# Two RMS norms of a transformer block computed from three sums gathered during the output projection, the second root applied behind the up and gate products

## What is computed

```python
mix = hybrid_mixer(rms_norm(h, g_pre_mix), ...)      # ends with merged @ w_out
h = h + rms_norm(mix, g_post_mix)
ffn = conv_gated_mlp(rms_norm(h, g_pre_ffn), w_up_gate, conv_w_ffn, w_down)
h = h + rms_norm(ffn, g_post_ffn)

def rms_norm(x, g):    # over the 1024 features of a token
    return x * rsqrt(mean(x * x) + 1e-6) * g

def conv_gated_mlp(xn, w_up_gate, conv_w_ffn, w_down):
    u, g = split(xn @ w_up_gate, 2)                  # 2 x 2816 features
    u = causal_dwconv(u, conv_w_ffn)                 # 3 taps along the tokens
    return (gelu(u) * g) @ w_down
```

## Time and profile before

| | us |
|---|---|
| median of 3 runs (1785.23 to 1788.03) | 1786.21 |
| the profiled execution, its own time | 1784.76 |
| its span | 1783.0 |
| PE, DVE, ACT, POOL busy | 1720.4, 1039.9, 877.9, 357.9 |
| last job of the output projection read by ACT | at 668.65 |
| first matmul of the up product | at 694.82 |
| end of the last up and gate product | at 946.16 |

### The profile page before, as it was taken

One profiled execution on the slowest core, in us unless ns is written; L12 is line 12 of the kernel. 1 busy time (PEld: TensorE's weight loads), 2 busy tenths in 40 slices (PEclk: granted clock), 3 DMA queues, 4 the chain that ended last, 5 costly groups with the idle time before them and its releaser, 6 DMA issues.

```text
span 1783.0 us, 29994 instructions
## 1 busy us (share of the span) xinstructions
PE 1720.4 (96%) x11496; PEld 1548.2 (87%) x11496; DVE 1039.9 (58%) x1589; ACT 877.9 (49%) x1205; POOL 357.9 (20%) x520
## 2 busy tenths in 40 slices
PE   6999999998999998999999998999999999999996
PEld 6999999998999998999998887788777777888885
DVE  6655566654455566875653336576677676755443
ACT  6777677775333243333333223475655555633331
POOL 0111101010000025988814970000000000000001
PEclk9999999999999997999999997999999999999998
DMA  4111222122444442443434544764112212233332
GB/s 154 61 56 57 72 71 71 60 60 66 137 154 162 160 149 42 142 135 109 122 103 133 141 111 163 210 199 128 48 60 89 65 53 82 77 106 112 119 115 90
DMA packets 67942, 189.22 MB, mean 106 GB/s; under 512 B 15248, under 2 KB 19472, under 8 KB 67728
## 3 DMA queue, kind: packets, MB, share of 16 engines
q1 hardware_dynamic: 63936, 175.99, 31.7%
q0 software_dynamic: 3920, 12.06, 2.4%
HBM read 165.74 MB, written 19.92 MB: 104 GB/s over the span
## 4 chain that ended last, share of the span: by engine, by line
PE 85%; DVE 6%; ACT 4%; issue 2%; DMA 1%; SPq 0%; POOL 0%; ACTq 0%; DVEq 0%
PE J L883 34%; PE J L1132 18%; PE J L899 7%; PE J L1102 7%; PE J L1267 2%; PE J L1257 2%; PE J L1006 2%; PE Z L923 2%; PE J L1312 2%; PE Z L978 1%; DMA WR<-weights 1%; DVE MX L2416 1%; DVE WL L1870 1%; PE Z L968 1%; PE Z L991 1%
## 5 line engine op out<-in xcount | busy, mean ns | idle before, releaser
L1870 DVE TENSOR_TENSOR WL<-WR,WH 128x1024 fp32r<-128x1024 f32 x247 | 326.2, 1327 | 224.2 <-ACT WH L1396 215.9
L1396 ACT ACTIVATE WH<-WR 128x1024 fp32r<-128x1024 f32 x247 | 259.6, 1055 | 229.3 <-DMA WR<-weights 115.1
L883 PE MATMUL J<-XH,WH 128*128 128x258 f32 (+1 forms) x1376 | 282.0, 286 | 4.6 <-ACT XH L1432 2.0
L883 PE MATMUL J<-XH,WL 128*128 128x258 f32 (+1 forms) x1376 | 279.0, 284 | 0.0
L883 PE MATMUL J<-XL,WH 128*128 128x258 f32 (+1 forms) x1376 | 273.8, 283 | 0.0
L883 PEld LDWEIGHTS J<-XH,WH 128*128 128x128 f32 x1376 | 216.4, 191 | 9.3 <-issue 6.8
L883 PEld LDWEIGHTS J<-XH,WL 128*128 128x128 f32 x1376 | 214.2, 190 | 0.0
L883 PEld LDWEIGHTS J<-XL,WH 128*128 128x128 f32 x1376 | 212.0, 189 | 0.1
L2558 POOL TENSOR_TENSOR SA<-SQ 128x512 f32<-128x512 f32 (+1 forms) x3 | 4.9, 1620 | 688.9 <-ACT SQ L1655 493.3
L2540 POOL TENSOR_SCALAR_AFFINE_SELECT E<-E 128x128 f32<-128x128 f32 (+2 forms) x160 | 48.2, 338 | 386.8 <-DVE E L1954 223.9
L1954 DVE SCALAR_TENSOR_TENSOR E<-Z,E 128x1348 f32<-128x1348 f32 x16 | 25.0, 1562 | 85.3 <-ACT E L1468 85.3
(11 more groups left out here) (438 smaller groups left out, 4152.5 us busy)
## 6 DMA issues: line engine op xcount, KB each, us to landing
WR<-weights SPq DMA_DIRECT2D x247, 512.0 KB, 3.6
AW<-weights SPq DMA_DIRECT2D x24, 512.0 KB, 4.5
CPS<-cp_dram SPq DMA_DIRECT2D x8, 576.0 KB, 6.7
cp_dram<-CQR POOLq DMA_DIRECT2D x16, 144.0 KB, 3.0
cp_dram<-CQI POOLq DMA_DIRECT2D x16, 144.0 KB, 2.9
X<-tokens SPq DMA_DIRECT2D x4, 528.0 KB, 5.1
H<-tokens SPq DMA_DIRECT2D x8, 264.0 KB, 4.7
bp_dram<-BQR POOLq DMA_DIRECT2D x8, 256.0 KB, 2.3
```

The source lines that it names most:

```text
L883: mm = pe.matmul(o[:, 512 * h:512 * h + half], ws[:, s, w], xs[:, a:a + half], start=(k == 0 and i == 0 and part != WITH_LOW), stop=(k == ...
L1396: act.activation(WH[:, n % SPLIT, :], WR[:, n % RAW, :], ACT.Copy).then_inc(w_hi, 1)
L1870: dve.tensor_tensor(WL[:, n % SPLIT, :], WR[:, n % RAW, :], WH[:, n % SPLIT, :].bitcast(F32), ALU.subtract).then_inc(w_lo, 1)
```

## The change

Let f be the mixer's output with `g_post_mix` applied, and r1 the first root. The sum of squares of the new `H = h + r1*f` is sum(h*h) + 2*r1*sum(f*h) + r1*r1*sum(f*f). So three sums, and that of the squares without the gain for r1, are gathered while the output projection runs. `H` is then rounded with the gain `g_pre_ffn` but without the second root; the second root `R2S` multiplies u behind the up product (before the taps) and the output of the gelu (before it meets the gate product).

- SP loads `H` in four transfers of two tiles, all of them in turns 0 and 1.
- ACT in turn m of the output projection: `F` with the gain, square of the raw result into `FSQ[m]`, square of `F` into `GSQ[m]`, square of tokens into `HSQ` (two buffers).
- DVE in turn m: `F*H`, and from the second on an add to `SUM_FH`. POOL: three adds a turn in place of one.
- The up loop: `PP` is read out by DVE with the multiplication in place of ACT's copy; one more multiplication on DVE behind the gelu.

```diff
+H_SQUARES = ((), (0, 1), (2, 3), (4,), (5,), (6,), (7,), ())
...
-                sp.dma_start(H[:, m * L1:(m + 1) * L1], x_view[:, m]).then_inc(h_landed, 16)
+                if m < 2:
+                    for k in (2 * m, 2 * m + 1):
+                        sp.dma_start(H[:, 2 * k * L1:2 * (k + 1) * L1].rearrange("p (m t) -> p m t", m=2),
+                                     x_view[:, 2 * k:2 * k + 2]).then_inc(x_landed[k], 16)
...
-            last_squares(Q_MIX + DT - 1, HALFK)
+            pe.wait_ge(out_added, OUT_ADDED['f', DT - 2])
+            pe.wait_ge(fh_added, 6)
+            token_sums(SUM_F, KEPT, True, False, ZF)
+            pe.wait_ge(out_step, OUT_STEP['f2', DT - 1])
+            token_sums(FSQ[DT - 1], KEPT, False, True, ZF).then_inc(sums_made, 1)
+            pe.wait_ge(fh_added, DT)
+            token_sums(SUM_FH, KEPT, True, True, ZFH)
             spread(1, KEPT)
-            for m in range(DT):
-                sum_squares(Q_PREF + m, m == 0, m == DT - 1, HALFK)
-            spread(2, KEPT)
+            pe.wait_ge(fh_added, DT + 1)
+            token_sums(SUM_G, KEPT, False, True, ZG)
+            pe.wait_ge(out_added, OUT_ADDED['h', DT - 1])
+            token_sums(SUM_H, KEPT, False, True, ZH).then_inc(sums_made, 1)
...
                     real(n + 1, t + 1, WITH_HIGH)
+                    pe.wait_ge(t_ready, DT)
+                    spread(2, KEPT, RST2)
...
-                act.activation(halves(F[:, m * L1 + LIVE:(m + 1) * L1]), JK[t % 2], ACT.Copy)
+                j, g = JK[t % 2], PRM[:, g_mix + m:g_mix + m + 1]
+                f = F[:, m * L1 + LIVE:(m + 1) * L1]
                 if m == 0:
                     act.wait_ge(ada_done, 3 * DT)
-                square(Q_MIX + m, JK[t % 2], HALFK)
+                if m == DT - 1:
+                    act.activation(halves(FSQ[m][:]), j, ACT.Square).then_inc(out_step, 1)
+                    act.activation(halves(f), j, ACT.Identity, scale=g).then_inc(out_step, 1)
+                else:
+                    act.activation(halves(f), j, ACT.Identity, scale=g).then_inc(out_step, 1)
+                    act.activation(halves(FSQ[m][:]), j, ACT.Square).then_inc(out_step, 1)
+                act.wait_ge(out_step, OUT_STEP['f', m])
+                act.activation(GSQ[m][:], f, ACT.Square).then_inc(out_step, 1)
+                for k in H_SQUARES[m]:
+                    if k % 2 == 0:
+                        act.wait_ge(x_landed[k // 2], 32)
+                    if k > 1:
+                        act.wait_ge(out_added, OUT_ADDED['h', k - 1])
+                    act.activation(HSQ[k % 2][:], H[:, k * L1 + LIVE:(k + 1) * L1], ACT.Square).then_inc(out_step, 1)
...
             root(1, KEPT)
-            pre_norm_hi(Q_PREF, 2, 0)
+            for m in range(DT):
+                act.wait_ge(h_ready, m + 1)
+                act.activation(XH[:, m * L1 + LIVE:(m + 1) * L1], H[:, m * L1 + LIVE:(m + 1) * L1], ACT.Identity,
+                               scale=PRM[:, g_pref + m:g_pref + m + 1]).then_inc(xh_ready, 1)
+                if m == 4:
+                    root(2, KEPT, RST2)
+            act.wait_ge(r_spread, 3)
+            act.activation(halves(R2S[:]), spread_out(2, KEPT), ACT.Copy).then_inc(r2_copied, 1)
...
                 split_hi(n + 3)
-                act.wait_ge(job_done, val(as_lin(n) + 1))
-                if positive(3 * i):
-                    act.wait_ge(fconv_step, val(3 * i))
-                act.activation(halves(PP[:, 0:KEPT]), JK[as_lin(t) % 2], ACT.Copy).then_inc(read_out[t % 2], 1)
                 split_hi(n + 4)
...
                 split_lo(n + 3)
-                dve.wait_ge(sq_done, val(Q_MIX + m + 1))
+                k = slice(m * L1 + LIVE, (m + 1) * L1)
+                if m % 2 == 0:
+                    dve.wait_ge(x_landed[m // 2], 32)
+                dve.wait_ge(out_step, OUT_STEP['f', m])
+                link(dve.tensor_tensor(SUM_FH[:] if m == 0 else CT[:, 0:KEPT], F[:, k], H[:, k], ALU.mult))
+                if m == 0:
+                    dve.nop().then_inc(fh_added, 1)
+                else:
+                    dve.tensor_tensor(SUM_FH[:], SUM_FH[:], CT[:, 0:KEPT], ALU.add).then_inc(fh_added, 1)
+                    dve.wait_ge(fh_added, m + 1)
+                dve.wait_ge(out_step, OUT_STEP['f', m] if m == DT - 1 else OUT_STEP['f2', m])
                 dve.nop().then_inc(read_out[t % 2], 1)
+                if m == DT - 1:
+                    dve.wait_ge(out_step, OUT_STEP['g2', m])
+                    dve.wait_ge(out_added, OUT_ADDED['g', DT - 2])
+                    dve.tensor_tensor(SUM_G[:], SUM_G[:], GSQ[m][:], ALU.add).then_inc(fh_added, 1)
                 parameters(m)
...
+            dve.wait_ge(sums_made, 1)
+            dve.tensor_scalar(r1, ZF[0:w, 0:n], 1.0 / D, EPS, ALU.mult, ALU.add).then_inc(r_step, 1)
+            dve.wait_ge(r_step, 3)
+            dve.reciprocal(r1, r1).then_inc(r_step, 1)
+            def second_root():
+                dve.wait_ge(sums_made, 2)
+                link(dve.tensor_tensor(r2, r1, ZG[0:w, 0:n], ALU.mult))
+                link(dve.scalar_tensor_tensor(out=r2, in0=ZFH[0:w, 0:n], scalar=2.0, in1=r2, op0=ALU.mult, op1=ALU.add))
...
+                dve.reciprocal(r2, r2).then_inc(r_step, 1)
+            r = rooted(1, KEPT)
+            for m in range(DT):
...
+                dve.tensor_tensor(halves(tmp), r, halves(F[:, k]), ALU.mult).then_inc(t_ready, 1)
+                dve.wait_ge(t_ready, m + 1)
+                dve.tensor_tensor(H[:, k], H[:, k], tmp, ALU.add).then_inc(h_ready, 1)
+                if m == 2:
+                    second_root()
+            for m in range(DT):
+                k = slice(m * L1 + LIVE, (m + 1) * L1)
+                dve.wait_ge(xh_ready, val(DT + m + 1))
+                dve.scalar_tensor_tensor(out=XL[:, k], in0=H[:, k], scalar=PRM[:, g_pref + m:g_pref + m + 1],
+                                         in1=XH[:, k].bitcast(F32), op0=ALU.mult, op1=ALU.subtract).then_inc(xl_ready, 1)
 
             def up(i):
...
                 split_lo(n + 3)
+                dve.wait_ge(job_done, val(as_lin(n) + 1))
...
+                dve.tensor_tensor(halves(PP[:, 0:KEPT]), JK[as_lin(t) % 2], halves(R2S[:]), ALU.mult)\
+                   .then_inc(read_out[t % 2], 1)
...
                 taps(i, cw_ffn, FT, fconv_step, SEQ, META - LIVE)
                 split_lo(n + 4)
+                dve.wait_ge(gelu_done, val(i + 1))
+                dve.tensor_tensor(VT[:, 0:SEQ], VT[:, 0:SEQ], R2S[:, KEPT - SEQ:], ALU.mult).then_inc(gelu_scaled, 1)
                 dve.wait_ge(job_done, val(n + 2))
...
-            gather_squares(Q_MIX, SA1, KEPT)
+            for m in range(DT):
+                for kind, tiles, total in (("f", FSQ, SUM_F), ("g", GSQ, SUM_G)):
+                    if 0 < m < DT - 1:
+                        pool.wait_ge(out_step, OUT_STEP[kind + "2", m])
+                        if m > 1:
+                            pool.wait_ge(out_added, OUT_ADDED[kind, m - 1])
+                        pool.tensor_tensor(total[:], tiles[0][:] if m == 1 else total[:], tiles[m][:],
+                                           ALU.add).then_inc(out_added, 1)
+                if m:
+                    pool.wait_ge(out_step, OUT_STEP["h2", m])
+                    if m > 1:
+                        pool.wait_ge(out_added, OUT_ADDED["h", m - 1])
+                    pool.tensor_tensor(SUM_H[:], HSQ[0][:] if m == 1 else SUM_H[:], HSQ[m % 2][:],
+                                       ALU.add).then_inc(out_added, 1)
```

More of the change, by code:

```diff
@@ L96 @@
 LATERS = 816
[L100 removed]
+Q_PRE, Q_FFN, Q_PRE2, Q_LAT, Q_KV, Q_POST2 = 0, 8, 16, 24, 26, 28
 S2 = SEQ
@@ L121, with count_out @@
 PI_BELOW = float(np.nextafter(np.float32(np.pi), np.float32(0)))
+H_SQUARES = ((), (0, 1), (2, 3), (4,), (5,), (6,), (7,), ())
+def count_out():
+    steps, added = {}, {}
+    for m in range(DT):
+        for kind in ("f2", "f", "g2") if m == DT - 1 else ("f", "f2", "g2"):
+            steps[kind, m] = len(steps) + 1
+        for k in H_SQUARES[m]:
+            steps["h2", k] = len(steps) + 1
+    for m in range(1, DT):
+        for kind in ("f", "g", "h") if m < DT - 1 else ("h",):
+            added[kind, m] = len(added) + 1
+    return steps, added
+OUT_STEP, OUT_ADDED = count_out()
 class Lin:
@@ L287, in build @@
         RSTD = sb("RSTD", [P, 8], M2 + 3200)
+        RST2 = sb("RST2", [P, 8], M2 + 3232)
         PRM = sb("PRM", [P, NP], M2 + 3360)
@@ L330, in build @@
         SA1 = sb("SA1", [P, L1], M1 + 4224)
+        FSQ = [sb(f"FSQ{m}", [P, KEPT], U[1] + 4 * L1 * m) for m in range(DT)]
+        GSQ = [sb(f"GSQ{m}", [P, KEPT], U[0] + 4 * L1 * m) for m in range(DT)]
+        HSQ = [sb(f"HSQ{x}", [P, KEPT], M1 + 12704 + 4 * L1 * x) for x in range(2)]
+        SUM_F = sb("SUM_F", [P, KEPT], M1 + 4224)
+        SUM_H = sb("SUM_H", [P, KEPT], M1 + 6336)
+        SUM_FH = sb("SUM_FH", [P, KEPT], M1 + 8480)
+        SUM_G = sb("SUM_G", [P, KEPT], M1 + 8480 + 4 * L1)
```

(32 more changed lines are left out.)

42 lines of the change are left out of this document (24 added, 18 removed).

## The result

The changed kernel takes **1814.72 us** (1812.76 to 1819.59, 4 runs) against 1785.72 us (1784.89 to 1788.03, 4 runs) for the kernel before on the same chip: ratio 1.0164, 95% interval 1.0142 to 1.0187. It is slower by 29 us; 1808 was forecast, with a range from 1792 to 1822. Its profiled execution took 1812.76 us, 28.0 more than that of the kernel before.

What follows compares the result with a forecast made beforehand. PE was taken as the bound, except in the serial stretch around the norm, with DVE nearly full beside POOL in the early up loop. Sum: 1784.8 + 5.1 + 17 = 1806.9, plus 1.4 to the median: 1808 us, range 1792 to 1822.

Steps and rivals of the forecast that it cites:

- the first rival: Output projection and up loop both lose, as forecast: 1808 us, own range 1799 to 1820; chance 0.52.
- The projection: Output projection up to ACT's read of the last job: 11 us later, at 680 (bounds 675.5 and 689).
- Its first two parts: Output projection: turn 3 begins 4 us late; then four loops of 7.6 instead of 5.8 us add 7.2 us.
- the loop of ACT and POOL: Output projection: ACT's token square waits for POOL's third add; 6.8 us a turn, 7.6 with DVE's interference.
- the fifth rival: Output projection: PE, waiting every turn, gets 0.50 of its clock; 5.8 us jobs take 10, 1826 us; chance 0.08.
- Read-out to first tile: From ACT's last read in the projection to DVE's first norm tile: 9.3 us, now 4.55 (bounds 5.6 and 9.9).
- First tile to the end of the first up turn: Norm and first up turn: 23.5 us in place of 34.5 (bounds 23 and 25).
- The up loop: Beside POOL's inputs DVE's turn grows from 11.16 to 14.0 us; the loop loses 17 us (bounds 8 and 22).
- The third rival: Up loop: a turn is only 12.6 us, priced by the unstretched `FL` row; 1799 us; chance 0.15.
- The fourth: Up loop: 11.16 us is POOL's turn, the multiplications fill DVE's elastic waiting, loop stays 11.35; 1783 or 1777 us; chance 0.05.
- The second rival: Output projection keeps its pace, up loop still loses 17 us: 1794 us; chance 0.20.
- The signs that the prediction named: Projection `F` every 7 to 8 us, PE idle between jobs; some 33 us to first up turn's end; gate products 13 to 15.

Runs made afterwards that it cites:

- Experiment 4: Changed kernel, but in the output projection ACT itself releases the PSUM buffer behind its square instead of DVE; 1814.27 us, ratio 1.0142.
- Experiment 11: Changed kernel without DVE's F*H products and adds of tiles 1 to 7, POOL's adds from the third tile cut to 8 columns; 1795.09 us, ratio 1.0047.
- experiments 1 and 3: Each against the changed kernel: 1 applies second root ahead of products, old up loop, 1803.19 us; 3 replaces POOL's 48 input operations by short fills, 1798.32 us.

## Why the prediction was right, and where its terms were off

**Sign, places and order of size** were right: both places lose (the first rival, given 0.52), and what is removed from the norm is less than what is put elsewhere. By the prediction's own count of the profiled execution, 22.1 us were forecast and 28.0 came. The two places were not sized alike: up to the end of the first up turn 5.1 were forecast and 13.5 measured, in the loop 17 and 14.9, and the second error hid 2.1 of the first's 8.4.

**The projection: 11 forecast, 17.7 measured, the term that was mis-sized.** Its first two parts held roughly. Turn 3 is 5.9 us late, 4 taken; the loop of ACT and POOL turns in 7.2 us, 7.6 taken. The sentence that failed is "PE isn't slowed further: with two `J` buffers it waits for ACT and DVE, which are already late". I priced DVE only as a guest in ACT's loop, 2.6 us of work that falls partly between POOL's adds. I didn't add up DVE's own turn beside POOL: `WL` 2.0, product 1.5, add 1.5 and the block of parameters, whose small operations wait for POOL as well. That turn is 9.9 us. DVE slides behind turn by turn, and in the last one it hands the buffer back 5.5 us late. Experiment 4 takes this release away: its turns are (680.47 - 650.73) / 4 = 7.4 us, and its 680.47 is the 680 of the forecast. The other 2 us of the last turn are the clock: at a granted 0.76 the last job takes 7.8 us instead of 5.8. So the fifth rival is true in small, in one job and not, as it had it, 10 us in every turn.

**Read-out to first tile: 9.3 forecast, 11.4 measured**, above my bound of 9.9. The operations are the forecast ones, but DVE came late to them: when the last `F` was ready, at 687.6, it was still at the add of tile 6, and a `WL` stood next, over at 689.9. It is the same omission, DVE's backlog. Experiment 11, with DVE's products gone, has 5.6, the lower bound. (The terms give 5.5 and 10.0 as bounds, where 5.6 and 9.9 were said.)

**First tile to the end of the first up turn: 23.5 forecast, 23.4 measured** (697.76 to 721.15). Every row had a counterpart of equal shape in the trace of before, and POOL's products began only at 715.19. That the sum holds to 0.1 us is luck all the same: the pairs and the second root took 12.0 us, not 13.1, and PE's tail of high passes 710.58 to 716.01, 5.4 and not 4.2; the granted clock was 0.50 from 701 to 713.

**The up loop: 17 forecast, 14.9 measured.** The turn is 13.8 us, forecast 14.0; POOL needs 83.6 us (715.19 to 798.80), forecast 92 and 88.4 before, so that fewer turns fall under it: 5 times 13.8 - 11.35, or 12.2 us, in place of 15.5. POOL wasn't slowed, as I thought it would be: its 48 tensor operations take 67.6 us together, against 72.4 before, and its issues (0.58 us each) and pauses (4.5 us in all against 4.8) are about as long as before. That a longer turn of DVE puts fewer collisions into POOL's way per microsecond would explain it, but isn't shown. The third rival's price, by the `FL` row, is refuted: `VT`'s product takes 1638 ns there, and three of five `FL` rise from 693 to 1471, the other two to 1148. The fourth, that 11.16 us was POOL's turn and the two multiplications would fill elastic time, falls with the turn of 13.8 and experiments 1 and 3: DVE's row is the one that sets the turn, and it sets it only while POOL computes.

The second rival, a projection that keeps its pace at 1794 us, is nearly what experiment 11 made by leaving work out: 1795. The signs that the prediction named came: `F` every 7.2 us but for the last, PE idle between jobs, 721.15 - 686.38 = 34.8 us from the last read to the end of the first up turn (33 said), gate products 12.8 to 14.6 apart.

The Trainium skill's rule (page "SBUF — State Buffer", section Who interferes with whom) agrees with the rows of `VT`'s product: with two SBUF inputs it takes 1638 ns beside POOL, 678 with one of them in PSUM, 810 with POOL's operations of the inputs gone. For one SBUF input the page excepts operations in a 2-port mode, and the prediction left the exception out. The first tap, with its one SBUF input, took 1296 ns beside POOL in the kernel before and 488 without (900.77 to 946.16), and 544 beside POOL in the changed one; whether it ran in such a mode isn't shown.

## What to carry to other kernels

Before work is put on an engine whose rows look short and whose idle time looks long, add up that engine's whole turn at the lengths that its operations have beside the neighbour that will run then, and ask who stands behind it in the queue; an idle 22 us elsewhere says nothing. Waits that were moved, a buffer released earlier and a changed order brought 1.1 to 4.5 us each at the first tile here, and 0.5 to 3.2 us in the time, because the engine behind them was full: take out work, or its collisions, first. And before repairs, price the ceiling by leaving the added work out: here it was 0.3%, and that run would have been the first to make.
